# Loading the gates of a dense expert sum for eight tiles at once instead of four

## What is computed

```python
def block(xt):                                    # 128 tokens at a time
    q = (xt @ wq).reshape(128, 8, 2, 128)
    ...                                           
    top, pos = lax.top_k(cand, 16)                # 16 experts per head, of 128 x 128
    eidx = jnp.take_along_axis(cidx, pos, axis=-1)
    g = jax.nn.softmax(top, axis=-1)
    u = expert_u[eidx]
    act = jax.nn.gelu(jnp.einsum("td,thkd->thk", xt, u), approximate=False)
    w = (act.astype(jnp.float32) * g).astype(xt.dtype)
    return jnp.einsum("thk,thkd->td", w, expert_v[eidx])
```

## Time and profile before

| | |
|---|---|
| median of 3 runs | 1787.14 us (1783.83 to 1787.2) |
| the profiled execution | 1788.47 us, its span 1786.7 us |
| TensorE busy | 1674.8 us, 94% of the span, mean granted clock 0.948 |
| VectorE, ScalarE, GpSimd busy | 1196.8, 603.6, 1076.0 us |
| read from and written to HBM | 358.15 MB and 54.53 MB |
| q1, the queue of SP's loads and stores | 131168 packets, 253.33 MB, 40.2% of 16 engines |
| q0, the queue of the gathers | 36864 packets, 134.23 MB, 21.6% of 16 engines |

### The profile page before, as it was taken

The page is one execution under the profiler, slowest core; times in us unless marked ns, Lnnn a source line. Parts: engine busy times, 40 slices in busy tenths (PEclk is TensorE's granted clock), DMA queues, the critical chain, the costliest instruction groups (busy, mean ns, idle before and its releaser), DMA issues. The chain is left out here.

```text
span 1786.7 us, 26267 instructions
## 1 busy us (share of the span) xinstructions
PE 1674.8 (94%) x9133; PEld 1494.9 (84%) x9133; DVE 1196.8 (67%) x2525; ACT 603.6 (34%) x862; POOL 1076.0 (60%) x542
## 2 busy tenths in 40 slices
PE   6998999869989989799999999979999999999978
PEld 5797855867789989799999999968888888888848
DVE  6576464440097989895999999156676767766645
ACT  2122333111122332235556565332333333333241
POOL 4552200235336867586666666569898988988622
PEclk9998955989999999999999999989999999999989
DMA  4121000132036878686899999889999999999631
GB/s 187 71 95 48 24 24 1 48 133 95 24 125 205 298 261 271 213 288 221 314 342 354 343 339 338 292 318 359 355 354 368 357 360 352 357 365 355 220 141 48
DMA packets 169835, 413.63 MB, mean 232 GB/s; under 512 B 12832, under 2 KB 95392, under 8 KB 164512
## 3 DMA queue, kind: packets, MB, share of 16 engines
q1 hardware_dynamic: 131168, 253.33, 40.2%
q0 software_dynamic: 36864, 134.23, 21.6%
q10 hardware_dynamic: 1728, 25.17, 3.6%
HBM read 358.15 MB, written 54.53 MB: 231 GB/s over the span
## 5 line engine op out<-in xcount | busy, mean ns | idle before, releaser
L1045 POOL TENSOR_TENSOR s_lo<-s_raw,s_hi 128x1024 fp32r<-128x1024 f32 x224 | 537.8, 2402 | 220.4 <-ACT s_hi L1159 216.8
L1090 PE MATMUL s_psum<-hn_hi,s_hi 128*128 128x384 f32 x1024 | 350.6, 342 | 28.4 <-POOL s_lo L1045 28.4
L1159 ACT CAST s_hi<-s_raw 128x1024 fp32r<-128x1024 f32 x256 | 267.0, 1047 | 250.4 <-PE s_psum L1136 150.8
L1090 PE MATMUL s_psum<-hn_lo,s_hi 128*128 128x384 f32 x1024 | 345.2, 337 | 0.0
L1090 PE MATMUL s_psum<-hn_hi,s_lo 128*128 128x384 f32 x1024 | 345.1, 337 | 0.0
L1136 PE MATMUL s_psum<-s_hi,s_whi 128*128 128x512 f32 x768 | 300.1, 391 | 11.1 <-DVE s_wlo L1391 11.0
L1136 PE MATMUL s_psum<-s_lo,s_whi 128*128 128x512 f32 x768 | 299.8, 390 | 0.0
L1136 PE MATMUL s_psum<-s_hi,s_wlo 128*128 128x512 f32 x768 | 299.7, 390 | 0.0
L1079 POOL DMA_INDIRECT s_gtile<-in_v_t,s_v_row x128 | 221.0, 1727 | 25.0 <-issue 24.3
L1090 PEld LDWEIGHTS s_psum<-hn_hi,s_hi 128*128 128x128 f32 x1024 | 195.0, 190 | 31.3 <-POOL s_lo L1045 31.1
L1090 PEld LDWEIGHTS s_psum<-hn_lo,s_hi 128*128 128x128 f32 x1024 | 194.9, 190 | 0.0
(11 more groups left out here) (297 smaller groups left out, 2918.4 us busy)
## 6 DMA issues: line engine op xcount, KB each, us to landing
s_raw<-in_u_t SPq DMA_DIRECT2D x128, 512.0 KB, 4.9
s_raw<-in_v_t SPq DMA_DIRECT2D x128, 512.0 KB, 7.3
act_scratch<-s_acts SPq DMA_DIRECT2D x128, 192.0 KB, 4.3
gate_scratch<-s_gtile ACTq DMA_DIRECT2D x12, 2048.0 KB, 10.2
scores<-act_scratch SPq DMA_DIRECT2D x32, 768.0 KB, 7.3
scores<-gate_scratch SPq DMA_DIRECT2D x32, 768.0 KB, 10.9
m_w_raw<-in_w_in SPq DMA_DIRECT2D x12, 1024.0 KB, 4.8
r_w_raw<-in_w_q SPq DMA_DIRECT2D x8, 1024.0 KB, 4.8
```

The source lines that it names most:

```text
L1045: pool.tensor_tensor(lo[:, s, :], raw[:, s, :], hi[:, s, :].bitcast(F32), ALU.subtract).then_inc(lo_ready[s], 1)
L1090: last = pe.matmul(psU[:, s % 2, :], uu[:, s, d * P:(d + 1) * P], hh[:, d, P:T], start=(n == 0 and d == 0), stop=(n == 2 and d == DC - 1))
L1159: act.copy(hi[:, s, :], raw[:, s, :]).then_inc(hi_ready[s], 1)
```

## The change

The gates are loaded for eight tiles (two groups) in one transfer, in pieces of 8 x 32 x 4 = 1024 bytes. There are again two buffers, now twice as large: the first lies where both old ones lay, the second at the start of `hn_hi`, which is free in this part. Gates and activations have semaphores of their own. SP issues a gate load with the activations of every even group; VectorE takes the half that belongs to its group. The loops over two groups become loops over four, with the first and last rounds written out.

```diff
-        in_loaded, wg_ready, whi_ready, wlo_ready = (ring(n, 2) for n in ("in_loaded", "wg_ready", "whi_ready", "wlo_ready"))
+        in_loaded, g_loaded, wg_ready, whi_ready, wlo_ready = (
+            ring(n, 2) for n in ("in_loaded", "g_loaded", "wg_ready", "whi_ready", "wlo_ready"))
...
-        g_in = flat[:, 2 * UR * DT:4 * UR * DT].rearrange("p (a g i t) -> p a g i t", a=2, i=UR, t=GT)
+        g_in0 = flat[:, 2 * UR * DT:4 * UR * DT]
+        g_in1 = nc.alloc_sbuf_tensor_at("s_g_in1", [P, 2 * UR * DT], F32, offset=shared["hn_at"])[:, :]
+        g_in = [gi.rearrange("p (g i t) -> p g i t", i=2 * UR, t=GT) for gi in (g_in0, g_in1)]
...
-                sp.dma_start(g_in[:, par, :, :, :], gate_dram[:, :, bass.ds(g * UR, UR), :].rearrange("g p i t -> p g i t")).then_inc(in_loaded[par], 16)
+
+            def load_gates(g, par, used):
+
+                reached(sp, wlo_ready[1], used)
+                sp.dma_start(g_in[par][:, :, :, :], gate_dram[:, :, bass.ds(g * UR, 2 * UR), :].rearrange("g p i t -> p g i t")).then_inc(g_loaded[par], 16)
...
             load_weights(0, 0, 0)
+            load_gates(0, 0, 0)
             load_weights(1, 1, 0)
             load_values(0)
...
-            with sp.Fori(1, turns // 2) as i:
-                load_weights(2 * i, 0, i)
-                load_values(2 * i)
-                load_weights(2 * i + 1, 1, i)
-                load_values(2 * i + 1)
+
+            def load_four(g, n):
+                load_weights(g, 0, 2 * n - 1)
+                load_gates(g, 1, 2 * n - 2)
+                load_values(g)
+                load_weights(g + 1, 1, 2 * n - 1)
+                load_values(g + 1)
+                load_weights(g + 2, 0, 2 * n)
+                load_gates(g + 2, 0, 2 * n - 1)
+                load_values(g + 2)
+                load_weights(g + 3, 1, 2 * n)
+                load_values(g + 3)
+
+            load_four(2, 1)
+            with sp.Fori(2, turns // 4) as n:
+                load_four(4 * n - 2, n)
...
-            def weights(par, turn):
-
-                dve.wait_ge(in_loaded[par], 32 * turn)
+            def weights(par, turn, g_buf, g_turn):
+
+                dve.wait_ge(in_loaded[par], 16 * turn)
+                dve.wait_ge(g_loaded[g_buf], 16 * g_turn)
                 a4 = a_in[:, par, :, :].rearrange("p i (g t) -> p i g t", t=GT)
-                dve.tensor_tensor(a4, a4, g_in[:, par, :, :, :].rearrange("p g i t -> p i g t"), ALU.mult).then_inc(wg_ready[par], 1)
+                mine = g_in[g_buf][:, :, par * UR:(par + 1) * UR, :].rearrange("p g i t -> p i g t")
+                dve.tensor_tensor(a4, a4, mine, ALU.mult).then_inc(wg_ready[par], 1)
```

More of the change, by code:

```diff
@@ L1029, in _ @@
                 sp.dma_start(h[:, t, :], h_dram[t]).then_inc(h_loaded, 16)
-            with sp.Fori(1, turns // 2) as i:
-                load_weights(2 * i, 0, i)
-                load_values(2 * i)
-                load_weights(2 * i + 1, 1, i)
-                load_values(2 * i + 1)
+            def load_four(g, n):
[12 more added lines that the diff above has]
+                load_four(4 * n - 2, n)
+            g = turns - 2
+            load_weights(g, 0, turns // 2 - 1)
+            load_gates(g, 1, turns // 2 - 2)
+            load_values(g)
+            load_weights(g + 1, 1, turns // 2 - 1)
+            load_values(g + 1)
         @block.gpsimd
@@ L1396, in _ @@
                 if c == c0 + first_ones:
-                    weights(0, 1)
+                    weights(0, 1, 0, 1)
                 dot(c % U_RING, c // U_RING + 1, col(dots, c))
@@ L1423, in low_values, with group @@
                 dve.tensor_tensor(lo[:, UR - 1, :], raw[:, UR - 1, :], hi[:, UR - 1, :].bitcast(F32), ALU.subtract).then_inc(lo_ready[UR - 1], 1)
-            def group(g, par, turn, final=False):
+            def group(g, par, turn, g_buf, g_turn, final=False):
                 if not final:
-                    weights(par, turn)
+                    weights(par, turn, g_buf, g_turn)
                 add_row(g, 0)
@@ L1435, in group @@
                 add_row(g, 3)
[L1437 to L1441, removed]
+            group(0, 1, 1, 0, 1)
+            with dve.Fori(1, turns // 4) as n:
+                group(4 * n - 3, 0, 2 * n, 1, n)
+                group(4 * n - 2, 1, 2 * n, 1, n)
+                group(4 * n - 1, 0, 2 * n + 1, 0, n + 1)
+                group(4 * n, 1, 2 * n + 1, 0, n + 1)
+            group(turns - 3, 0, turns // 2, 1, turns // 4)
+            group(turns - 2, 1, turns // 2, 1, turns // 4)
+            group(turns - 1, 0, 0, 0, 0, final=True)
             dve.wait_ge(h0_loaded, 16)
@@ L1601, in block_kernel @@
         mixer(nc, shared, io)
+        shared["hn_at"] = nc.sbuf_base
         with ExitStack() as mid:
```

## The result

The changed kernel takes 1820.6 us (median of 6 runs, 1817.8 to 1824.11), the kernel before 1786.91 us (6 runs, 1783.83 to 1788.91): the ratio is 1.0195, 95% interval 1.0184 to 1.0205. It is slower by some 1.95%, far outside the range given. The profiled execution has a span of 1822.3 us, 35.6 us more than before.

A forecast was written before the change was run, and what follows sets the result against it. TensorE's own pace, 16.3 us a group, was taken as the bound, with nil margin at group 2. Terms -1.0 + 2.4 = +1.4 us gave a median of 1788.5 us from 1787.14; range 1784.5 to 1792.5.

The forecast's parts named there:

- Term 1: Start of the part: fewer gate pieces ahead of the first value tiles, 1.0 us gained, between 0 and 2.0.
- Term 2: Group 2: doubled gates land later, 2.4 us lost (0 to 4.2); TensorE's wait grows from 0.3 to 2.7 us.
- rival 1: The wait at group 2 also halves the clock for 3 us: +2.9, 1790.0 us, up to 1791.8; chance 0.24.
- the sum: Whole kernel: 1.0 us gained at the start, 2.4 lost at group 2, together +1.4 us.
- Term 3: Groups 3 and on: odd weights 4.2 us sooner, even ones 2.4 later, chain gains 1.8 a pair; costed at nothing.
- upper bound of 4.2: Group 2: most the doubled load could delay the gates, a gate load's whole step in the steady stretch, 4.2 us.
- Rival 2: Doubled load late at groups 4 and 6 too: +5.0 us, 1792.1 us; chance 0.06.
- the upper price: Groups 4 and 6: the doubled gate load takes 15.1 us to land, where 13.3 was forecast.
- Rival 3: DMA is the true limit, so 0.7 us a pair comes out: 10.5 us less, 1776.6 us; chance 0.04.
- The sign for group 2: One TensorE wait of 2 to 3.5 us before group 2, released by VectorE's low halves or the instruction beside them.
- q1 lower by some 11 us per engine: Profile sign: DMA time of q1 falls by some 11 us per engine, with gate loads 16 instead of 32.
- the line of 7 ns and 0.0387 ns a byte: DMA cost of a packet: 27 ns for 512 B, 47 ns for 1 KB, saving 0.7 us per engine a pair.

The follow-up runs named there:

- e1: Changed kernel with each eight-tile gate load issued one group earlier, ahead of the odd group's values: 1789.72 us, ratio 1.0021 against the kernel before.
- f1: Changed kernel with VectorE's low_values(g) moved ahead of the weights of group g + 1: 1812.81 us, ratio 1.0148 against the kernel before.
- f2: Changed kernel with low_values(g) ahead of the next weights, group 0's values ahead of group 1's activations, loads of h last: 1783.64 us, ratio 0.9999.

## Why the prediction was wrong

**What bounds the kernel: right, and not enough.** TensorE at 16.3 us a group was the limit. But the loop through SP and VectorE turned in 32.2 us beside TensorE's 32.6, and I never measured it. (Its own length may be less: ScalarE's casts, which stand in it, waited for TensorE 54 times there.) I read a margin from the weights of group 30, 6.8 us early, as if it could be spent; it had been built up at 0.4 us a turn. And "TensorE waits in two places of this part only" overlooks the third, for the low half in slot 3 at 1204.05, which is the one that grew.

**Term 1, the start: right.** First gap 9.36 us, a gain of 1.6 us where 1.0 was forecast. **Term 2, group 2: right in size.** The wait there is 3.05 us against 2.7. Only its place was off: ahead of slot 3 of group 1, for the low values. SP issued the gates 1.8 us sooner (1180.58) and they took 19.5 us to land, before 17.5. The clock fell behind the gap, so rival 1 came true as well. At the start of group 2 TensorE stood 1.7 us behind the kernel before (1210.05 and 1208.38), where the sum was +1.4, or +2.9 with the clock. So far the forecast held; nearly the whole 35.6 us came after it.

**Term 3 is the step that failed**: "The chain thus gains some 1.8 us a pair", costed at nothing. It was -4.2 + 2.4; measured -4.7 + 5.5 + 2.1 = +2.9 us a pair (32.2 to 35.1). The odd link was right within half a microsecond. The even link was more than double my 2.4, and over its upper bound of 4.2: the second half of the load added 4.9 us to the landing (10.9 to 15.8), where I had 1.9 us of DMA time and up to 1.0 for the gathers. The 2.1 us from product to next issue I had not priced at all: the freed odd product runs right behind the even group's work on VectorE, and the low half after it now falls beside GpSimd's (3.33 us for 1.22). I treated the wait of even groups and the gain of odd ones as separate margins, though they are links of one turn and only their sum decides.

**Rival 2 was the true one**, and undersized: it let the late load cost two groups, and counted on SP to come to it sooner. At group 4 SP did (1218.69, before 1220.80), but the load took 16.2 us, more than the upper price. Then each late product delays the next issue, and at group 8 SP comes later (1288.40, before 1285.81). An estimate from the turn, 2.5 us (35.1 - 32.6) over 14 or 15 turns, is 35 to 37.5 us. **Rival 3**, DMA as the limit, falls: with gathers left out and the engines 0.65 to 0.68 busy, the time is still 1782.6. The pieces do save DMA time: the gates' packets took 27.9 ns each before and 47.8 now, 12.2 us less per engine in all, 0.8 a pair where 0.7 was forecast. Nobody needed it.

**What the profile was to show.** The signs named for rival 2 (waits in later groups) and rival 1 (0.50 near 1205 us) both came. The sign for group 2, a wait released by the low halves "or the instruction beside them", held only by its second half. The sign "q1 lower by some 11 us per engine" failed: all of q1's packets took 717.7 us per engine before and 716.0 now, for its 4 KB packets took longer (186 ns in the values part, before 178). In e1 the fall is there, to 706.0.

## What to carry to other kernels

Where a queue's next load waits for a consumer that itself waits for the last load, add up the whole turn (issue to landing, landing to release, every link and every group in it) and compare it with the pace of the bounding engine; a margin seen far downstream is only what has gathered at a small difference per turn. Merging two loads makes the first of them late by what the second adds to the landing under the traffic that is really there (here 4.9 us); issue it earlier, or let each consumer wait for its own part. And try the start of a part alone: here moving the loads of group 1 behind the first values, with the loads of h put last, won 0.3%, and made the difference in one pair of kernels (f1 and f2) between a loop that fell behind and one that didn't.

## What the runs showed of the hardware

- 786 KB more in a gate load cost 4.9 us of landing time in the traffic of this part (10.9 to 15.8 us); without the gathers the whole 1.5 MB landed in 10.4.
- A packet of 512 B took 27.9 ns and one of 1 KB 47.8 ns of a DMA engine, so the line of 7 ns and 0.0387 ns a byte (27 and 47) held.
- Gaps of 1.83, 2.19, 2.40, 2.74 and 3.05 us were followed by 3.4 us at 1.2 GHz, gaps of 1.94 and 2.01 us were not.
- VectorE's 128x1024 subtraction took 1.22 us in all 32 groups before, where it never fell beside GpSimd's of the same size, and 2.48 to 3.33 us in the 15 groups of the changed kernel where it did for more than half a microsecond. In each of the 15 it ended 1.09 us after GpSimd's, which took its usual 2.4 us, as if most of it had run behind the other and not beside it.
- The same loop has two paces. With another start f1's ran without a gap, 28 us shorter in span (1808.5 and 1780.8).
